# GpSimd's order of gathers and TensorE's place for a tile's scores in a two-layer decoder with product-key experts

## The reference

```
q = (xb @ w_query)  ->  8 heads, 2 halves;   s = q . sub_keys        # 128 scores a half
top_s, top_i = top_k(s, 16);  cand = all 16 x 16 sums;  best 16 of them -> idx (of 16384), gate = softmax
u = expert_u[idx]                                     # 16 rows of 1024 per token and head
act = gelu(u . x);   w = gate * act
out = sum over heads and picks of w * expert_v[idx]   # 16 more rows of 1024
```

## Time and profile before

| | |
|---|---|
| median of 3 runs | 2034.05 us |
| the profiled execution's own time | 2032.86 us |
| its span, first to last instruction | 2031.0 us |
| granted TensorE clock, mean | 0.877 of full speed |
| gathers: q0 software_dynamic | 553.72 MB, 1056 gathers |
| all traffic | 616.74 MB, 304 GB/s over the span |
| GpSimd's DMA_INDIRECT, u rows | x528, mean 948 ns |
| GpSimd's DMA_INDIRECT, v rows | x528, mean 966 ns |
| VectorE's dot, L1485 | x528, mean 1216 ns |
| TensorE's mix, L842 | x1968 matmul records, mean 649 ns |

### The profile page before, as it was taken

One profiled execution on the slowest core, in us unless ns is written; L12 is line 12 of the kernel. 1 busy time (PEld: TensorE's weight loads), 2 busy tenths in 40 slices (PEclk: granted clock), 3 DMA queues, 4 the chain that ended last, 5 costly groups with the idle time before them and its releaser, 6 DMA issues.

```text
span 2031.0 us, 14496 instructions
## 1 busy us (share of the span) xinstructions
PE 1564.5 (77%) x4050; PEld 723.2 (36%) x4050; DVE 1096.4 (54%) x2706; ACT 365.4 (18%) x948; POOL 1039.9 (51%) x1110
## 2 busy tenths in 40 slices
PE   8999986797776665869878875697878766666777
PEld 3477644352222222424333422243335222222222
DVE  2433245545555555466666556556675565555541
ACT  1032202121111111221121211211112111111100
POOL 1110033555556666447466565456665566566663
PEclk9955697899899987889889997798989988989899
DMA  4211035998888888779999998799999888888896
GB/s 169 86 42 59 24 130 223 402 325 338 329 332 331 337 345 342 279 270 376 405 351 410 398 347 325 294 354 418 416 362 343 330 331 341 331 342 343 344 382 243
DMA packets 184126, 616.74 MB, mean 304 GB/s; under 512 B 19275, under 2 KB 20811, under 8 KB 184054
## 3 DMA queue, kind: packets, MB, share of 16 engines
q0 software_dynamic: 152064, 553.72, 70.5%
q1 hardware_dynamic: 31990, 62.17, 8.3%
HBM read 614.77 MB, written 1.05 MB: 303 GB/s over the span
## 4 chain that ended last, share of the span: by engine, by line
PE 34%; DVE 19%; issue 14%; POOL 13%; another core or an unknown queue 9%; DMA 8%; DVEq 2%; ACT 1%; SPq 0%; POOLq 0%
POOL arena L568 13%; PE bank L644 11%; PE bank L842 10%; DMA arena<-peer_u,idx 6%; DVE arena L1485 4%; PE bank L745 3%; PE bank L816 2%; PE bank L717 1%; DVEq L381 1%; PE bank L977 1%; DMA arena<-peer_v,idx 1%; PE bank L706 1%; PE bank L633 1%; DVE pairs L1468 1%
## 5 line engine op out<-in xcount | busy, mean ns | idle before, releaser
L842 PE MATMUL bank<-arena 128*128 128x512 f32 x1968 | 1000.8, 649 | 291.8 <-DMA arena<-peer_v,idx 204.2
L1485 DVE CUSTOM_DVE_ANT_0 arena<-arena,bank 128x1024 f32<-128x1024 f32 x528 | 620.9, 1216 | 259.9 <-DMA arena<-peer_u,idx 232.4
L568 POOL DMA_INDIRECT arena<-peer_u,idx x528 | 500.7, 948 | 376.9 <-DVE dots L1485 181.7
L568 POOL DMA_INDIRECT arena<-peer_v,idx x528 | 510.1, 966 | 355.2 <-issue 152.3
L842 PEld LDWEIGHTS bank<-arena 128*128 128x128 f32 x1968 | 376.2, 204 | 872.5 <-issue 472.0
L644 PE MATMUL bank<-wring,hT 128*128 128x512 f32 (+5 forms) x604 | 264.2, 593 | 9.7 <-DVE gws L1552 9.3
L644 PEld LDWEIGHTS bank<-wring,hT 128*128 128x128 f32 (+1 forms) x604 | 110.7, 185 | 159.8 <-issue 156.1
L1131 ACT ACTIVATE arena<-con,wgt 128x128 f32<-128x128 f32 x492 | 149.5, 388 | 63.4 <-PE bank L842 30.3
L1443 DVE MAX8 top<-bank 128x8 f32<-128x128 f32 x66 | 16.4, 289 | 202.2 <-remote 98.0
L1122 ACT ACTIVATE gl<-dots 128x16 f32<-128x16 f32 x33 | 7.1, 216 | 620.9 <-issue 466.5
L533 POOL TENSOR_TENSOR small<-small,con 128x1 f32<-128x1 f32 (+3 forms) x11 | 7.5, 684 | 134.0 <-DVEq L1251 133.8
(11 more groups left out here) (157 smaller groups left out, 1072.5 us busy)
## 6 DMA issues: line engine op xcount, KB each, us to landing
wring<-gla_w_in SPq DMA_DIRECT2D x12, 2048.0 KB
arena<-peer_u,idx POOLq DMA_INDIRECT x528
arena<-peer_v,idx POOLq DMA_INDIRECT x528
wring<-gla_w_out SPq DMA_DIRECT2D x4, 2048.0 KB
wring<-peer_w_query SPq DMA_DIRECT2D x4, 2048.0 KB
wring<-attn_w_in SPq DMA_DIRECT2D x2, 2048.0 KB
wring<-attn_w_out SPq DMA_DIRECT2D x2, 2048.0 KB
gws<-peer_w_query SPq DMA_DIRECT2D x2, 2048.0 KB, 10.3
```

The lines of the kernel that those rows point to most:

```text
L568: nc.gpsimd.indirect_dma_start(out=ring[:, k % RING, :], out_offset=None, in_=table.rearrange("l e d -> (l e) d"), in_offset=bass.Indirect ...
L842: last = nc.tensor.matmul(yacc[:, 512 * i:512 * i + 512], wdiag[:, k, :], vrow[:, k % RING, 512 * i:512 * i + 512], start=first, stop=last ...
L1485: v.tensor_tensor_reduce(out=urow[:, k % RING, :], in0=urow[:, k % RING, :], in1=xnow, scale=1.0, scalar=0.0, op0=ALU.mult, op1=ALU.add, a ...
```

## The change

On GpSimd, u(i, k) now stands ahead of the v row beside it, and the v rows trail by LEAD = 4 picks: at pick k of turn i it issues u(i, k), then v(i-1, k-4), or for k under 4 v(i-2, k+12), the last four rows of the tile before (none in turn 2). After the last turn the last four v rows of tile 32 follow. On TensorE `scores(i+2)` moves from the end of turn i to behind mix 11 (and behind a chunk at pick 11, where there is one). Nothing else changes; each engine does the same work.

```diff
+LEAD = 4
@@ GpSimd, turns 2 to 33
                 for k in range(TOPK):
-                    gather(1, i - 1, k)
                     if i < TILES:
                         gather(0, i, k)
+                    if k >= LEAD:
+                        gather(1, i - 1, k - LEAD)
+                    elif i > 2:
+                        gather(1, i - 2, TOPK - LEAD + k)
                     if k == 11 and i in STAGES:
                         for t in STAGES[i][0]:
                             mixer_root(t, STAGES[i][1])
                     if k == 11 and i == 26:
                         root(small[:, 1:2], small[:, 4:5], 1)
+            for k in range(TOPK - LEAD, TOPK):
+                gather(1, TILES - 1, k)
             root(small[:, 2:3], small[:, 5:6], 1)
@@ TensorE, each turn
                     if i in STAGES and k in CHUNKS_AT[(i - 2) % PH]:
                         next(chunks)
+                    if k == 11 and i + 2 < TILES:
+                        scores(i + 2)
                 assert next(chunks, None) is None
-                if i + 2 < TILES:
-                    scores(i + 2)
```

## The result

The changed kernel takes 2126.84 us (median of 4 runs, 2121.23 to 2134.76) against 2034.09 us of the kernel before beside it (4 runs, 2025.77 to 2037.19): ratio 1.0466 [1.0419, 1.0512]. The forecast was 2069 us with a range up to 2105: right in sign, wrong in size. The span of the profiled execution is 2126.5 us, 95.5 more than before, where +36 had been forecast.

A forecast was written before the change was run, and what follows sets the result against it. The prediction took ordinary turns to be bound by a loop of gathers, dots, weights and choice, stretched by late semaphores. Its terms, 32 + 18 - 20 + 3 + 3 = +36, gave 2069 us, range 2002 to 2105.

The forecast's parts named there:

- 13 ordinary turns: Turns without mixer stage: scores told late, so the choice starts some 13 us after the weights; +2.5 us each, +32.
- block ends: Turns 9, 17, 25: VectorE's add before the choice waits for v(i-1,15), now sent later; +6 us each, +18.
- mixer turns: Scores ahead of the last mixes, v rows no longer holding u rows: -12 first pass, -8 second, -20 together.
- up to turn 3's first dot: Turn 2: gelu waits for the last query behind TensorE's mixes, and v(1,4) leaves behind u(2,8); +3 us.
- last turn: After the last weights up to two rows of tile 31 are still unmixed; +3 us.
- Rival A: Posts not delayed by place in TensorE's line: ordinary turns 0, block ends +9, mixer -20, ends +6; 2028 us, chance 0.22.
- VectorE's shares: Mixer turns: VectorE's adds of v(i-1,4), (8), (12) before dots 4, 8, 12 get later rows; 0 to 3 us in few turns.
- What the mixer turns gain: Part on mixer turns: scores stand before the last mixes, 5 to 12 us earlier, and v(10,11) no longer holds u rows.
- the gain of 20 us: Mixer turns: -12 us in the first pass and -8 in the second; bounds together -45 to 0.
- Every sign: Ordinary turns 50 us or more, choice 10 us late, first dots of 10, 18, 26 late, turn 10's choice prompt, v(10,11) unheld.
- Rival B's freed ring: Mixer turns lose half their DMA holes as u no longer stands behind v: -35 to -45 us, 2008 us, chance 0.20.
- Rival C: Scores and block ends wait for GpSimd's hole every time: 16 turns x 6 = +96, less 14; 2115 us, chance 0.08.

The follow-up runs named there:

- after_fourth: The changed kernel run again, unaltered, on a quick chip: 1882.42 us, ratio 1.028 to the kernel before.
- after_late_add: The changed kernel with the block-end add of the finished sum behind VectorE's next choice, quick chip: 1854.36 us, ratio 1.010 to the kernel before.
- after_shares_chunks6: The changed kernel with VectorE adding picks 0, 4, 8 ahead of dots 5, 9, 13 and turns 15 and 23's query chunks earlier: 1857.5 us, ratio 1.011 (again 1.014).
- after_three: The changed kernel with scores behind mix 7 (11 in turns 15, 23), VectorE's shares at picks 0, 4, 8 and earlier query chunks, slow chip: 2024.32 us, ratio 0.988.
- after_again: The changed kernel run again, unaltered, on a slow chip: 2125.13 us, ratio 1.044 to the kernel before.
- early scores and the early choice: Kernel before with scores behind mix 7 and choice of tile i+2 between turn i's dots 10 and 11 (turns 15, 23: mix 11, dot 15): ratios 0.941, 0.944.
- all four edits: The changed kernel with scores behind mix 7, shares at picks 0, 4, 8, earlier query chunks and late block-end add, slow chip: 2004.33 us, ratio 0.986.

## Why the prediction was wrong

The terms, forecast against first-dot times of the two traces:

| term | forecast | measured |
|---|---|---|
| 13 ordinary turns | +32 | +35.2 |
| block ends, turns 9, 17, 25 | +18 | +22.9 (7.4, 7.7, 7.8) |
| mixer turns | -20 | +29.3 (turns 10 to 14 -2.6, 15 +15.7, 18 to 22 -0.1, 23 +16.3) |
| up to turn 3's first dot (forecast: turn 2) | +3 | +1.3 (turn 2 +11.7, turn 1 -6.6, the part ahead of it -3.8) |
| last turn | +3 | +6.8 |
| sum | +36 | +95.5 |

Ordinary turns: right in mechanism, and in size as far as it holds still. The choice starts 10.6 to 17.4 us after the weights in 12 of 13, and where posts are quick turn 5 of the same kernel takes 40.1 us. Their sum was 679.9, 679.0 and 666.7 us in three profiles on slow chips, so the term is some +19 to +35. Rival A was right in kind, but of other chips: there ordinary turns cost nothing. It fell all the same, at 1.028, since its other terms were as wrong as mine.

Block ends: right; on the slow chip +7.6 each, 1.6 more than taken. For posts without delay I gave +3; after_fourth shows 50.7 to 50.9 against the 42.3 to 42.8 of after_late_add, 8 us. The error: with posts at once the turn is as short as issue allows, 40 us, so the add's wait has no slack to hide in; I had set it against a turn that already contained slow posts.

Mixer turns: this step failed, by 49 of the 59.5 us missing. Three things in it were wrong.

The first is the price of VectorE's shares. The forecast let v(i-1,12) leave 21.25 us after u(i,8), took the weights to be possible about 35 us after the first dot, and put that at 0 to 3 us in a few turns and at nothing in the sum. Measured, v(i-1,12) leaves 22.4 to 28.7 us after u(i,8), because in eight of the twelve turns u(i,12) first waits 3 to 6 us for dot(i,4), and the last dot ends at 35.5 to 44.8 us, past 40 in nine turns. In turns 14, 20, 21 and 22, where gelu follows the dots at once, that is 9 to 12 us a turn. They lost 19 us together, although the wait for scores was gone or halved.

The second is "in most mixer turns they come later anyway, because ScalarE or a stopped GpSimd is late". I took ScalarE's lateness as fixed. It isn't: in turns 15 and 23 gelu stands behind copies of what TensorE's chunks make, and every chunk stands in TensorE's queue behind a mix whose v row I had moved by four picks. "What the mixer turns gain" counted the scores, which moved forward, and not the chunks, which moved back with the rows. There nothing was gained, as the scores' wait had been 1.4 and 1.8 us, and 17 to 18 us were lost.

The third is the gain of 20 us itself. The waits for scores did shrink, as forecast, but in turn 10 the 8.4 us gained behind the weights were lost ahead of them, and turns 10 to 14 and 18 to 22 came out at -2.6 and -0.1.

after_shares_chunks6 takes 22.5 us out of the mixer turns on a quick chip. That the shares and the chunks make the whole +49 on a slow chip isn't shown; after_three, with the scores' move too, has mixer turns 52 us shorter than after_again on the same chip, but turns 15 and 23 there are still 11 and 12 us longer than before the change. What holds these two stays open; in the changed kernel late posts have a part in them (61.8 against 52.5 us to gelu).

Every sign that the forecast had named for itself came true: turns of 50 us or more, the choice 10 us or more behind the weights in most, block ends late by 7.4 to 7.8 us, turn 10's choice at once behind the weights, v(10,11) without its wait (0.30 us). None of them looked at the dots or at gelu of a mixer turn, so none could show this failure.

Up to turn 3 the near hit is luck. Turn 2 alone took 11.7 us more, not 3: gelu, behind the last query's copy, stands 55.9 us after the first dot instead of 42.6. Turn 1 was 6.6 us shorter and the part ahead of it 3.8, which the forecast didn't have.

The last turn: +6.8 for +3, of the right kind. Not two but five rows of tile 31 are unmixed behind the last weights: TensorE mixes 21 rows in 36.3 us there, where the earlier trace rows has 16 in 27.7.

Rival B's freed ring brought nothing: v gathers wait 137 us less, but u gathers wait for dots, and those for the shares and the choice. Rival C's price came close to the total (2115) for the wrong reason: it laid 96 us on ordinary turns and block ends, which took 58.

The Trainium skill (DMA: Bandwidth & Descriptors, Anatomy of one DMA) gives about 100 ns for the semaphore update that ends a DMA; for posts from engine to engine it gives none there. TensorE's post to VectorE takes as long on the quick chip (0.1 us), and not on the chip of the result (12.1 us).

The Trainium skill (VectorE: DVE Perf Modes, the section on the trn2 errata) asks to space out dense increments because increments at a high rate from one engine can deadlock another. No run here hung, and no run here varies the increments; the same program with the same increments has the delay in some sessions and not in others.

## What to carry to other kernels

When rows are moved in a queue, list for each later engine everything that stands in its queue behind a consumer of these rows, not only their direct consumers: here mixer chunks, then copies, then gelu. A chain that one wait hides on another engine is no cover if that wait hangs on the same moved rows. Where a small chain of semaphores closes the loop from one tile to the next, take it off the loop before trimming it: on slow chips early scores and the early choice together gave 6%, where the new order with all four edits gave 1.4%. And name a sign of failure for each term of a forecast, the ones put at nothing above all.

## What the runs showed of the hardware

- The same kernel took 1835.35, 1835.48 and 1828.11 us in three sessions and 2034.09, 2036.13 and 2030.58 in three others, each with runs within 1% of one another. The five sessions of the experiments had a chip each. The changed kernel costs 2.8% in the first kind (one session) and 4.4 to 4.8% in the second. Whether it is the chip, and why, stays open.
- In the second kind a post from TensorE to VectorE took 12.1 us (turn 5 of the changed kernel), and one of VectorE to itself 4.02 to 5.76 us (after_three), while gathers were issued without a pause; in 12 of 13 ordinary turns the late one came within 3.7 us of the moment at which GpSimd stopped. Not every post is late there: in turn 10 of the kernel before TensorE's took 0.1 us (859.35 to 859.45), 7.5 us after GpSimd had taken up issuing again. In the first kind, with 420 GB/s of the same gathers, it takes 0.1 us. So the delay is not a matter of the gathers' rate alone.
